# A 33-turn expert loop: gathered rows written already turned, biases laid out in four row groups, four held weight units, and loads placed ahead of it

## The reference, cut to what matters

```python
logits = h @ w_router + b_router              # (256, 32)
top_val, top_idx = lax.top_k(logits, 4)
gates = softmax(top_val)
# for each expert e, over the tokens that chose it:
u   = h[tok] @ w1[e] + b1[e]                  # (n, 2048)
glu = minimum(u[:, 0::2], 7.0)
lin = clip(u[:, 1::2], -7.0, 7.0)
act = glu * sigmoid(1.702 * glu) * (lin + 1.0)
y   = act @ w2[e] + b2[e]                     # (n, 1024)
out[tok] += gate * y
```

## Time and profile before

| | us |
|---|---|
| median of three runs | 2665.75 |
| the profiled execution, its own time | 2661.23 |
| its span | 2658.4 |
| TensorE busy | 2544.8 |
| VectorE busy | 924.9 |
| ScalarE busy | 583.4 |

### The profile page before, as it was taken

The page is one execution under the profiler, slowest core; times in us unless marked ns, Lnnn a source line. Parts: engine busy times, 40 slices in busy tenths (PEclk is TensorE's granted clock), DMA queues, the critical chain, the costliest instruction groups (busy, mean ns, idle before and its releaser), DMA issues.

```text
span 2658.4 us, 42182 instructions
## 1 busy us (share of the span) xinstructions
PE 2544.8 (96%) x18014; PEld 1673.4 (63%) x18014; DVE 924.9 (35%) x2004; ACT 583.4 (22%) x1168; POOL 149.5 (6%) x124
## 2 busy tenths in 40 slices
PE   8999999999999999999997889899999999999998
PEld 6867878888884887888886777433333333333333
DVE  1863363312277245323476653311111111111112
ACT  2100233301100123220135433311111111111112
POOL 0050000000032000000003220000000000000000
PEclk9999999999999999999999999999999999999999
DMA  7555232344455422336410002999999999999995
GB/s 262 198 182 198 100 122 98 124 158 159 175 204 176 173 95 96 127 128 214 162 64 4 4 4 108 420 428 428 428 428 429 428 428 427 429 428 428 429 427 251
DMA packets 135029, 636.13 MB, mean 239 GB/s; under 512 B 5120, under 2 KB 5392, under 8 KB 109136
## 3 DMA queue, kind: packets, MB, share of 16 engines
q1 hardware_dynamic: 133904, 629.78, 59.6%
q0 software_dynamic: 992, 4.37, 0.5%
HBM read 633.08 MB, written 1.05 MB: 239 GB/s over the span
## 4 chain that ended last, share of the span: by engine, by line
PE 94%; ACT 2%; DVE 2%; issue 1%; DMA 1%; SPq 0%; ACTq 0%; DVEq 0%
PE bank L268 26%; PE bank L2601 17%; PE bank L2629 9%; PE bank L459 6%; PE bank L1405 4%; PE bank L481 4%; PE bank L289 4%; PE bank L1356 4%; PE bank L2563 2%; PE bank L2592 2%; PE bank L2549 2%; PE bank L1664 1%; PE bank L357 1%; PE bank L2621 1%; ACT hidT L2712 1%
## 5 line engine op out<-in xcount | busy, mean ns | idle before, releaser
L268 PE MATMUL bank<-hT,ring 128*128 128x256 f32 x3136 | 689.8, 380 | 2.5 <-DMA ring<-in_w_in 1.4
L268 PEld LDWEIGHTS bank<-hT,ring 128*128 128x128 f32 x3136 | 592.8, 190 | 94.6 <-issue 13.3
L2601 PE MATMUL bank<-ring,hsel 128*64 128x512 f32 x2112 | 462.0, 595 | 0.0
L2601 PEld LDWEIGHTS bank<-ring,hsel 128*64 128x64 f32 x2112 | 149.0, 137 | 310.8 <-issue 310.5
L2874 DVE TENSOR_SCALAR glu<-bank 128x256 f32<-128x256 f32 x66 | 28.0, 425 | 754.2 <-PE bank L2601 750.9
L2629 PE MATMUL bank<-ring,hidT 128*64 128x512 f32 x1024 | 226.8, 595 | 22.0 <-ACT hidT L2712 22.0
L754 DVE SCALAR_TENSOR_TENSOR a_buf<-v_pad,par,a_buf 128x256 f32<-128x256 f32 x480 | 215.8, 529 | 0.0
L2629 PEld LDWEIGHTS bank<-ring,hidT 128*64 128x64 f32 x1024 | 70.5, 137 | 156.2 <-issue 128.1
L1405 PE MATMUL bank<-ring 64*64 64x64 f32 (+1 forms) x5696 | 133.3, 229 | 25.6 <-issue 9.3
L1405 PEld LDWEIGHTS bank<-ring 64*64 64x64 f32 x5696 | 120.9, 137 | 40.6 <-issue 12.1
L2703 ACT ACTIVATE sig<-glu 128x256 f32<-128x256 f32 x66 | 27.5, 417 | 458.8 <-DVE glu L2874 458.8
(11 more groups left out here) (435 smaller groups left out, 2467.6 us busy)
## 6 DMA issues: line engine op xcount, KB each, us to landing
ring<-in_w SPq DMA_DIRECT2D x196, 2048.0 KB, 16.7
ring<-in_w_in SPq DMA_DIRECT2D x66, 2048.0 KB, 7.8
ring<-in_w_ada SPq DMA_DIRECT2D x12, 2048.0 KB, 8.0
ring<-in_w_ret_out SPq DMA_DIRECT2D x8, 2048.0 KB, 7.8
ring<-in_w_out SPq DMA_DIRECT2D x6, 2048.0 KB, 8.6
ring<-in_w_conv_out SPq DMA_DIRECT2D x4, 2048.0 KB, 8.3
ring<-in_w_attn_out SPq DMA_DIRECT2D x4, 2048.0 KB, 8.0
extra<-in_w SPq DMA_DIRECT2D x2, 2048.0 KB, 34.7
```

The costliest lines, as they stand in the source:

```text
L268: mm = nc.tensor.matmul(out[:, j, :], w[:, k, col + j * P:col + (j + 1) * P], rhs[:, k, :], start=(k == 0), stop=(k == DC - 1))
L2601: mm = nc.tensor.matmul(half(flat[4 + b], side), g["hsel"][:, 2 * (j % 2) + k, j // 2, :], w[:, at:at + UNIT], start=False, stop=(j == 3 a ...
```

## The change

The gather now holds a 128 x 128 piece of `h_tok` still (every fourth feature) and moves `sel` (64 columns) past it, 16 products for each job, so that the result has features in the partitions at once. `gsel`, the four transposes and one copy on ScalarE go. The biases lie in four groups of 32 partitions, each group with a quarter of the columns, so the four bias products of a job use four different groups of rows of the array; the gates are turned into four copies for the same layout. `extra` holds four units of expert 16 (2 to 5) in place of two. Unit 4 of expert 16 and unit 4 of expert 0 are loaded once the last step over tokens is staged; three others are issued earlier than before too. Memory is laid out again to make room, and four small tiles of the mixer move from `squares` to `m_k` under the name `gn_sq`. The diff, cut:

```diff
@@ mixer_loads
+    sp.wait_ge(g["staged"].sem, g["staged"].at(2 * STEPS - 1, 1))
+    moe_unit(sp, moe, KEPT, 4, moe["extra"][4]).then_inc(moe["extra_in"].sem, moe["extra_in"].one())
+    moe_unit(sp, moe, 0, 4, moe["slots"][4]).then_inc(moe["e_landed"][4].sem, moe["e_landed"][4].unit)
     sp.wait_ge(g["y_kept"].sem, g["y_kept"].at(STEPS - 1, 1))
@@ mixer_tensor, mixer_scalar, mixer_vector
-        nc.tensor.matmul(flat[4 + n], blk64, g["squares"][:, n, :], start=True, stop=True).then_inc(
+        nc.tensor.matmul(flat[4 + n], blk64, g["gn_sq"][:, n, :], start=True, stop=True).then_inc(
...
@@ moe_memory
-    sb("b2", [D], parts=N_EXPERTS)
-    sb("b1", [2 * D_FF], parts=N_EXPERTS)
+    sb("b2", [D // GROUPS])
+    sb("b1", [2 * D_FF // GROUPS])
...
-    extra = sb("extra", [2, DC * UNIT])
-    g["extra"] = {4: extra[:, 0], 5: extra[:, 1]}
+    extra = sb("extra", [4, DC * UNIT])
+    g["extra"] = {2: extra[:, 0], 3: extra[:, 1], 4: extra[:, 2], 5: extra[:, 3]}
@@ moe_loads
-    for j in (1, 2, 0):
-        if j == 2:
-            sp.wait_ge(g["mo_done"].sem, g["mo_done"].at(None, 4))
-        unit(0, j, g["slots"][j]).then_inc(landed(j).sem, landed(j).unit)
-    for dst, what in (("grids", g["grids_dram"]), ("b2", g["b2_dram"][0]), ("b1", g["b1_dram"][0])):
-        sp.dma_start(g[dst][:, :], what).then_inc(g["late_in"].sem, g["late_in"].one())
-    for j in (3, 4, 5):
-        unit(0, j, g["slots"][j]).then_inc(landed(j).sem, landed(j).unit)
-    for j, s in zip((4, 5), g["extra_in"]):
-        unit(KEPT, j, g["extra"][j]).then_inc(s.sem, s.one())
+    first(1)
+    kept(3)
+    sp.wait_ge(mixer["cat_ready"].sem, mixer["cat_ready"].at(None, 2))
+    kept(5)
+    sp.wait_ge(g["mo_done"].sem, g["mo_done"].at(None, 2))
+    first(2)
+    sp.wait_ge(g["mo_done"].sem, g["mo_done"].at(None, 4))
+    first(0)
+    sp.dma_start(g["grids"][:, :], g["grids_dram"]).then_inc(g["late_in"].sem, g["late_in"].one())
+    for name, width in (("b2", D // GROUPS), ("b1", 2 * D_FF // GROUPS)):
+        for q in range(GROUPS):
+            sp.dma_start(g[name][q * N_EXPERTS:(q + 1) * N_EXPERTS, :],
+                         g[name + "_dram"][0, :, q * width:(q + 1) * width]).then_inc(g["late_in"].sem, g["late_in"].one())
+    first(3)
+    first(5)
+    sp.wait_ge(g["x_part"].sem, g["x_part"].at(None, DC))
+    kept(2)
...
-    job(KEPT, range(4))
+    job(KEPT, range(2))
@@ moe_tensor
     for t in range(TC):
-        mm = nc.tensor.transpose(flat[7][0:N_EXPERTS, t * P:(t + 1) * P], g["gate_map"][:, t, 0:N_EXPERTS], ident)
+        for q in range(GROUPS):
+            mm = nc.tensor.matmul(flat[7][q * N_EXPERTS:(q + 1) * N_EXPERTS, t * P:(t + 1) * P], g["gate_map"][:, t, 0:N_EXPERTS],
+                                  ident, start=True, stop=True)
...
+        for i in range(2):
+            for q in range(GROUPS):
+                lo, hi = q * N_EXPERTS, (q + 1) * N_EXPERTS
+                nc.tensor.matmul(g["bank"][q][:, i, :], g["b2"][lo:hi, i * P:(i + 1) * P], g["gT"][lo:hi, :],
+                                 start=(i == 0), stop=False, skip_group_check=True)
@@ gather, turn_gathered
-        for t in range(TC):
-            for side in range(2):
-                mm = nc.tensor.matmul(half(flat[6], side), g["sel"][:, t, :], g["h_tok"][:, t, side * UNIT:(side + 1) * UNIT],
-                                      start=(t == 0), stop=(t == 1))
-        return mm
-
-    def turn_gathered():
         for c in range(4):
-            mm = nc.tensor.transpose(flat[6][:, c * P:(c + 1) * P], g["gsel"][:, c::4], ident)
+            for j in range(2):
+                for t in range(TC):
+                    mm = nc.tensor.matmul(flat[6][:, (2 * c + j) * SLOTS:(2 * c + j + 1) * SLOTS],
+                                          g["h_tok"][:, t, j * UNIT:(j + 1) * UNIT][:, c::4], g["sel"][:, t, :],
+                                          start=(t == 0), stop=(t == 1))
         return mm
@@ job
         for b in range(2):
             for side in range(2):
-                at = (2 * side + b) * UNIT
-                nc.tensor.matmul(half(flat[4 + b], side), g["bsel"][0:N_EXPERTS, :], g["b1"][:, at:at + UNIT], start=True, stop=False)
+                lo, hi = (2 * side + b) * N_EXPERTS, (2 * side + b + 1) * N_EXPERTS
+                nc.tensor.matmul(half(flat[4 + b], side), g["bsel"][lo:hi, :], g["b1"][lo:hi, :], start=True, stop=False)
...
-        pe.wait_ge(g["ga_out"].sem, g["ga_out"].at(t, 1))
-        turn_gathered().then_inc(g["gb_done"].sem, g["gb_done"].one())
@@ moe_scalar, in the loop
         act.wait_ge(g["ga_done"].sem, g["ga_done"].at(t, 1))
-        take_gathered().then_inc(g["ga_out"].sem, g["ga_out"].one())
+        take_rows().then_inc(g["gt_out"].sem, g["gt_out"].one())
         act.wait_ge(g["st_done"].sem, g["st_done"].at(t, 1))
         nc.scalar.activation(g["selgT"][:, :], flat[7][:, 0:T], ACT.Copy).then_inc(g["st_out"].sem, g["st_out"].one())
-        act.wait_ge(g["gb_done"].sem, g["gb_done"].at(t, 1))
-        take_rows().then_inc(g["gt_out"].sem, g["gt_out"].one())
```

More of the change, by code:

```diff
@@ L2325 @@
 EXTRA = 16
+GROUPS = P // N_EXPERTS
 JOBS = N_EXPERTS + EXTRA
@@ L2372, in moe_signals @@
         g[name] = follow(hyb[spent], DEPTH * hyb[spent].per + base, per)
-    g["extra_in"] = [follow(g["start_in"], g["start_in"].per, 1), Signal(ctx, nc, "extra_in", 1, 16)]
+    g["extra_in"] = Signal(ctx, nc, "extra_in", 4, 16)
 def moe_memory(ctx, nc, g):
@@ L2393, in moe_memory @@
         sb(name, [TC, JOBS])
-    sb("top", [TC, 8])
-    sb("few", [TC, 4])
     for name in ("tally", "over", "ends"):
         sb(name, [N_EXPERTS])
-    sb("before", [EXTRA, N_EXPERTS])
-    sb("onehot", [EXTRA, N_EXPERTS])
-    sb("work", [EXTRA, N_EXPERTS])
     sb("which", [EXTRA])
@@ L2405, in moe_memory @@
     sb("jobs", [JOBS], mybir.dt.int32)
-    sb("gT", [T], parts=N_EXPERTS)
     sb("sel", [TC, SLOTS])
-    sb("selg", [TC, 2, SLOTS])
-    sb("bsel", [SLOTS])
-    sb("selgT", [T])
-    sb("gsel", [4 * P])
     sb("hsel", [4, 2, SLOTS])
-    sb("glu", [2, 2 * P])
-    sb("lin", [2, 2 * P])
-    sb("sig", [2, 2 * P])
-    sb("hid", [4 * P])
-    sb("hidT", [4, 2, SLOTS])
-    sb("ye", [4 * P])
-    sb("finrow", [2, T])
-    sb("tiles", [T])
-    extra = sb("extra", [2, DC * UNIT])
-    g["extra"] = {4: extra[:, 0], 5: extra[:, 1]}
+    sb("tiles", [T])
+    sb("spot", [3])
+    g["extra"] = {2: extra[:, 0], 3: extra[:, 1], 4: extra[:, 2], 5: extra[:, 3]}
+    g["h3"] = shared[:, :].rearrange("p (c t) -> p c t", c=DC)
+    for i, name in enumerate(("before", "onehot", "work")):
+        g[name] = shared[:, i * GRID:(i + 1) * GRID].rearrange("p (o e) -> p o e", o=EXTRA)
+    for i, name in enumerate(("glu", "lin", "sig", "hid")):
+        g[name] = shared[:, i * 4 * P:(i + 1) * 4 * P]
+        if name != "hid":
+            g[name] = g[name].rearrange("p (b f) -> p b f", b=2)
     g["fin"] = g["h3"]
+    g["grids"] = turned
+    g["hidT"] = turned[:, 0:4 * P].rearrange("p (c h s) -> p c h s", c=4, h=2)
+    g["finrow"] = turned[:, 4 * P:8 * P].rearrange("p (a t) -> p a t", a=2)
 def moe_turns(eng, g):
@@ L2453, in moe_loads, with first, kept @@
-    for j, s in zip((4, 5), g["extra_in"]):
-        unit(KEPT, j, g["extra"][j]).then_inc(s.sem, s.one())
+    def first(j):
+        moe_unit(sp, g, 0, j, g["slots"][j]).then_inc(landed(j).sem, landed(j).unit)
+    def kept(j):
+        moe_unit(sp, g, KEPT, j, g["extra"][j]).then_inc(g["extra_in"].sem, g["extra_in"].one())
+    first(1)
[3 more added lines that the diff above has]
+    sp.wait_ge(g["mo_done"].sem, g["mo_done"].at(None, 2))
```

92 lines of the change are left out of this document (45 added, 47 removed).

## The result

| | before | after |
|---|---|---|
| median of 4 runs each, us | 2664.9 | 2918.6 |
| profiled execution: span, us | 2658.4 | 2914.7 |
| TensorE busy, us | 2544.8 | 2782.6 |
| PEld busy, us | 1673.4 | 1926.2 |

The changed kernel is slower by 9.5%: the ratio of its time to that of the kernel before is 1.0954, with a 95% interval of [1.0935, 1.0973]. The ratios further down are each against runs of the kernel before that were taken along with the experiment (medians 2665.17, 2664.84 and 2667.57 us for the three groups of experiments). I had said 2712 and 2688 to 2765. The direction was right and the size was not: 254 us more, where I forecast 46.6.

The account below looks back on a forecast made before the run. TensorE's unbroken chain bounds the loop, 28.76 us per job, transfers close behind. Gather +2.32 and bias -0.87 give +1.45 per job, +47.9 over 33; with -1.3 ahead, +46.6 on 2665.75 gives 2712 us, range 2688 to 2765.

Parts of the forecast that it names:

- Gather: Gather in each expert-loop job: 32 records at 0.12 us plus 0.2 for changing array parts, 4.04 us, +2.32 per job.
- The clock: Rival, chance 0.08: each light gather brings a half-clock stretch on TensorE, 33 x 1.5 = 50 us more, 2762 in all.
- Bias: Bias products of each job: four row groups run at once, 1.86 us becomes 0.99, -0.87 per job.
- the sums of `b2`: Ahead of the loop: 16 records four at a time take 1.07 us; with the first gather 5.11, -1.3 us.
- Removed transposes worth 0: The four `gsel` transposes, 0.48 us per job: TensorE waits for ScalarE's copy to the same moment instead, worth 0.
- Loads ahead of the loop, bound -1 to +1: Loads moved ahead of the expert loop, with SP's new waits: bound 0 to -1 or +1 us, taken as 0.
- The two bounds 6 us apart: Loop's end before the change: transfers end about 2628.5, last unit wanted at 2634.5, so TensorE's gain alone is worth little.
- Four held units worth 0: Held units and loads ahead take five units, 24.5 us, out of a stream nobody waits for any more: worth 0.

Follow-up runs that it names:

- the two runs: Changed kernel with the old gather put back: two early loads inside the last step over tokens, 2662.47 us, against the same loads issued behind `w_out2`, 2651.43 us.

## Why the prediction was wrong, point by point

- **Gather: the step that failed.** "so do the transposes of `gsel`, and they take 0.48/4 = 0.12 us per record" was a true reading, and the wrong price for this gather. The new gather holds every fourth column, and so do those transposes, but a transpose is a single record of another kind: the two loads with adjacent columns (L2614) take 0.20 us with a mean of 0.14, so they start 0.06 apart, so 0.12 was the doubled price of a transpose. An fp32 product's record costs 0.11 with adjacent columns and twice that with a distance of 16 bytes. I had both rows and took their closeness, 0.11 and 0.12, for agreement, where one had the distance in it and the other had not. 7.66 - 4.04 = 3.62 us per job is 119 us in 33, and the first gather, ahead of the loop, takes 3.7 more too (7.73): 123. What the runs show: adjacent columns 3.71, 8 bytes 3.91, 16 bytes 7.66 for 32 records. The Trainium skill, "SBUF — State Buffer", section "Door 1: The DMA port swizzle (why `[64,N]` ≈ `[32,N]`)", has the rule that I did not draw on: a line of this memory is 16 bytes, and reads keep full pace only with at least two of them in the same line. By that, two fp32 values 8 bytes apart share a line and two 16 bytes apart do not, and the traces agree: 0.122 and 0.239. The same section of the Trainium skill says that one can stride 4 fp32 for free; here that is the case that costs double.
- **The clock: a rival with the right mechanism, and too low a chance.** I gave it 0.08, with the reason that a gather is no idle time. The fall comes without any idle time, from light work: 64 columns moved in 0.233 us. It is tied to the failed step, since at 0.116 us per record (adjacent columns) it does not appear. My price was 50 us on top. By the run with 128 moved columns it is 2918.6 - 2840.9 = 78: I had 1.5 us for each job, and it is 2.46, since the scatter, the turn and in every fifth job the second weight product fall into the slow stretch. The rival's total of 2762 missed by 157 all the same, as it stood on the 4.04.
- **Bias: right.** 0.99 forecast, 1.02 measured, in all runs with it; the sums of `b2` were forecast at 1.07 and are 1.07 to 1.08 where both halves stand together and the clock is 1.00. Four products of 32 rows run at once, though two of them write one bank. The Trainium skill, "TensorEngine Tiling (Array Packing)", section "Gotcha 1: PSUM Pressure", would have kept it at 1.86; the trace does not agree, for the two halves of a bank.
- **Removed transposes worth 0: right.** In place of 0.48 us stands the wait for ScalarE's copy, 2051.76 to 2052.22.
- **Loads ahead of the loop, bound -1 to +1: wrong.** I asked who waits for these loads, and nobody does. What I did not ask is what they disturb. The step beside them got 7.8 us longer with the old gather and 6.9 in the changed kernel (1588.43 to 1627.66, against 32.3). Of the 7.5 us between the two runs, 4.7 lie at the two long "issue" pieces, in which TensorE waited for nothing that the profile shows, and 2.4 in the small products behind them, which ran at half clock. That the fetch of instructions competes with the 2 MB transfers is the reading that fits, and fewer instruction packets in those 10 us speak for it; what was shown is that moving the two loads out of the step takes the lost time away.
- **The two bounds 6 us apart: wrong, and without effect on the forecast.** At unit 3 of the last job it was 0.7 us. For the last unit it was 4 and not 6: its load is issued at 2609.46 and lands 21.1 us later, at 2630.5, not at the 2628.5 that I took from the DMA share. The room decides what a gain on TensorE is worth: 2 to 6 of 28 us, as the grouped biases alone show.
- **Four held units worth 0: right for the changed kernel,** as far as its trace tells: no wait in its loop ends with a transfer. No run took them out of it. With the old gather two of them are worth about 3 us by the traces, and by the times no difference is shown.

The sum again: 46.6 forecast, 123 for the load of the held columns, 78 for the clock, 7 for the step: 255, where 254 were measured. The terms are not known that well, since the 78 rest on a single run.

The best version is the one without the new gather and with the early loads behind `w_out2`: 2651.4 us, 0.5% under the kernel before; with job 17's loads in order it is 2649.0, which is not shown to be faster. It keeps the biases, the held units and three of the earlier loads.

## What to carry to other kernels

When a price is taken from a row of the old kernel, match the kind of instruction and the access pattern one at a time: look for the same kind with the other pattern, and the same pattern with the other kind, before two close numbers are called agreement. If a product holds many columns for few moved ones, lay the held operand out so that its columns are at most 8 bytes apart, and ask whether the array then has enough to do to keep its clock. Ask of a transfer that nobody waits for what runs beside it, and of a gain on one engine which unit the other bound wants first.

## What the runs showed of the hardware that I had not expected

- Loading 128 fp32 columns for one record of a product, at a granted clock of 1.00: 0.116 us at 4 bytes of distance, 0.122 at 8, 0.23 at 16; and 0.06 against 0.12 for a transpose, by the starts of its loads.
- The pace of the 16-byte load does not depend on TensorE's clock: the records of the gather are 0.233 us apart at 1.00 and at 0.50, and the first gather, all of it at 0.50, takes 7.73. The load of adjacent columns does depend on it, 3.71 for the gather at 1.00 and 7.05 at 0.50, and the scatter goes from 1.93 to 3.72.
- The granted clock fell with TensorE busy all the time, and stayed up when each record moved 128 columns in place of 64.
- Two loads of 2 MB beside a step of many short instructions made that step some 7 us longer (38.2 to 39.9 us against 31.6 to 32.5 in eleven traces), with TensorE idle under "issue" and then at a granted clock of 0.50.
- Four products of 32 rows, two of which write one bank in different halves, took 1.02 us where the same four in one row group took 1.86.
